# The gate row moved ahead of the scatter for the last two experts of a mixture-of-experts tail

## The chip, the cores and the metric

The kernel runs on one core of a Trainium2 chip. A core has TensorE (PE in the profile, with its weight loads as PEld), VectorE (DVE), ScalarE (ACT), GpSimd (POOL) and SyncE (SP, which issues DMAs), each with a queue of its own that it works off in order. Matmuls write into eight PSUM banks of 128 partitions by 512 floats; everything else lies in SBUF. The metric is the device time of one execution in microseconds.

## The reference, cut to what matters

The model is a two-layer hybrid block on 256 tokens of width 1024, and behind it a second block that ends in a mixture of experts with 16 experts, of which each token uses two. Only the end of it is touched here:

```
x = x + g_f[:, None] * _hier_moe(hf, ...)      # the last operation of the program

out = jnp.zeros_like(t)
for e in range(N_EXPERTS):
    hid = jax.nn.silu(t @ w1[e]) * (t @ w3[e])
    out = out + gate[:, e:e + 1] * (hid @ w2[e])
```

`gate[:, e]` is one number per token and expert. `g_f` is one row of 1024 numbers, the same for every token; the kernel holds it, laid over all partitions, in `gab[:, 1, :]`, and it is called the gate row here. (In the trace `gab` has the name `lnb`, since it shares that buffer.) Since the row doesn't depend on the token, it may be multiplied in before or after rows are handed back to their tokens.

## The kernel before, in words

Every matrix product is made in three matmuls of 32-bit halves: an operand is split into a rounded part (suffix h) and the rest (suffix l), and high by high, low by high and high by low are added in a bank (lines 842, 843 and 844). ScalarE makes the high part of each weight half (line 1602), VectorE the rest (line 2273). The weights stream in through SyncE in a fixed order.

The experts run in chunks, two to an expert (c = 0 to 31, expert x = c // 2). `Walk.experts` sets the order of the work for all engines alike: for a chunk the up products, then the transposed hidden rows of the chunk before (`turn_hidden`, written as `Pall` in the trace), then the down product of the chunk before (`down_part`).

- The first 14 experts (`NFAR`) take their own packed 128 tokens. Their rows go from the bank by ScalarE to `Y[x % 2]`, and GpSimd sends them with an indirect DMA to `ydram`. After chunk 28 GpSimd fetches every token's two possible rows from there (`far`, which is `arena` and `memT` in the trace).
- The last two experts (14 and 15) don't go through DRAM. ScalarE copies the bank to `Yp[0]` (Yph in the trace), VectorE subtracts that from the bank into `Yp[1]` (Ypl), and `scatter(x)` hands both to the tokens by matmuls with a one-hot matrix `back` (line 1566), eight for each expert, into banks 0 to 3: bank 2·hf + t holds columns hf·512 on, of token tile t. Both experts add up in the same banks.
- `combine(t)`, called once behind `down(29)` and once behind `down(30)`, weights and adds the fetched rows of token tile t: ScalarE scales `far[t]` (line 1586), VectorE multiplies and adds (line 2252, the form with two tensors of 128x1024 in SBUF), and GpSimd multiplies by the gate row (line 3327) and adds to `h` (line 3329).

At the end, VectorE multiplies each of the four banks by the gate row into `arena` ("fin"). For the two right halves it adds the product to `h` itself, for the two left halves GpSimd does (line 3333). SyncE stores the four quarters of `h` (line 3413) as they come.

Each engine runs its own queue in the order in which the code is written for it. On VectorE the stretch that matters is: rest of expert 14's rows, `combine(0)`, `Pall` of chunk 30, first half of the last weight tile (`P0l`), hidden rows of chunk 31, second half of `P0l`, `combine(1)`, `Pall` of chunk 31, rest of expert 15's rows, the end.

## Time and profile before

| | us |
|---|---|
| median of 3 runs | 1546.87 (1546.45 to 1547.77) |
| the profiled execution's own time | 1544.67 |
| span of its profile | 1542.9 |
| PE busy in the span | 1515.6 (98%) |
| DVE busy | 1170.5 (76%) |
| ACT busy | 937.8 (61%) |
| POOL busy | 81.0 (5%) |

The span runs from the first to the last thing that the profiler recorded; 1.8 us of the execution lie around it. The stretch that the change touches is the last 26 us, 1517 to 1543. In a timeline a row gives the start and the time of one or several like instructions, and in brackets how long the engine had been idle before it and who ended that. A duration holds the time from issue to end, so an instruction that is held up after it was issued shows as a long one.

### The profile page before, as it was taken

The page shows a single profiled execution, that of the slowest core. Times are in us where ns is not written, and L with a number is a line of the kernel's source. Part 1 is how long each engine was busy: PE and PEld are TensorE (multiplying, and loading weights), DVE is VectorE, ACT ScalarE, POOL GpSimd, SP SyncE. Part 2 cuts the span into 40 slices and gives each one's busy share as a digit, 9 for nine tenths or more (in the row PEclk, how much of TensorE's full clock was granted, in tenths as well). Part 3 has the DMA queues.
Part 4 walks back from the last instruction along what each step waited for, and adds up shares of the span by engine and source line. Part 5 has one row for each costly group of instructions (what it writes and reads, how often), then busy time and mean ns, then how long its engine had stood idle before and what let it go on. Part 6 is the DMA issues. An engine that isn't in the chain of part 4 may idle for free.

```text
span 1542.9 us, 20001 instructions
## 1 busy us (share of the span) xinstructions
PE 1515.6 (98%) x7856; PEld 1257.2 (81%) x7856; DVE 1170.5 (76%) x1623; ACT 937.8 (61%) x1487; POOL 81.0 (5%) x78
## 2 busy tenths in 40 slices
PE   9999999999999999999999999999999889999997
PEld 9988888888888799888888888887777678888785
DVE  7448866667878683688576689886677789999998
ACT  6468854655444354778547554544355468888884
POOL 0010000001000000100000000000200000000005
PEclk9999999999999999999999999999999999999999
DMA  7535345436776444553454468984521349999994
GB/s 294 209 116 215 141 157 195 160 137 260 260 271 246 164 161 168 191 192 137 157 198 178 150 229 316 335 322 161 191 103 55 143 185 367 370 381 384 360 370 169
DMA packets 52200, 339.33 MB, mean 220 GB/s; under 512 B 7835, under 2 KB 8477, under 8 KB 13316
## 3 DMA queue, kind: packets, MB, share of 16 engines
q1 hardware_dynamic: 48932, 331.79, 57.9%
q0 software_dynamic: 3168, 6.20, 1.1%
q8 instruction: 64, 1.05, 0.3%
q14 instruction: 36, 0.29, 0.1%
HBM read 332.82 MB, written 10.49 MB: 223 GB/s over the span
## 4 chain that ended last, share of the span: by engine, by line
PE 88%; DVE 8%; ACT 2%; issue 1%; DMA 1%; POOL 0%; SPq 0%; DVEq 0%; ACTq 0%; POOLq 0%
PE bank L842 25%; PE bank L844 25%; PE bank L843 25%; PE bank L848 5%; DVE wls L2273 2%; PE bank L990 2%; PE bank L1181 1%; PE bank L1379 1%; PE bank L1159 1%; DVE h L2243 1%; PE bank L1098 1%; DMA raw<-in_ws_dram 1%; PE bank L1121 1%; DVE arena L2252 1%; ACT whs L1602 1%
## 5 line engine op out<-in xcount | busy, mean ns | idle before, releaser
L2273 DVE TENSOR_TENSOR wls<-raw,whs 128x1024 fp32r<-128x1024 f32 x424 | 504.2, 1225 | 165.4 <-ACT whs L1602 164.4
L1602 ACT ACTIVATE whs<-raw 128x1024 fp32r<-128x1024 f32 x424 | 427.6, 1051 | 198.6 <-PE bank L844 161.8
L842 PE MATMUL bank<-whs,P1h 128*128 128x512 f32 (+1 forms) x732 | 290.4, 397 | 2.0 <-issue 2.0
L844 PE MATMUL bank<-whs,P1l 128*128 128x512 f32 (+1 forms) x732 | 284.4, 389 | 0.0
L843 PE MATMUL bank<-wls,P1h 128*128 128x512 f32 (+1 forms) x732 | 283.6, 387 | 0.0
L842 PE MATMUL bank<-whs,P0h 128*128 128x512 f32 (+1 forms) x632 | 251.7, 398 | 1.4 <-DVE P0l L2243 1.4
L844 PE MATMUL bank<-whs,P0l 128*128 128x512 f32 (+1 forms) x632 | 245.1, 388 | 0.0
L843 PE MATMUL bank<-wls,P0h 128*128 128x512 f32 (+1 forms) x632 | 244.5, 387 | 0.0
L842 PEld LDWEIGHTS bank<-whs,P1h 128*128 128x128 f32 x732 | 137.6, 188 | 29.7 <-issue 3.3
L844 PEld LDWEIGHTS bank<-whs,P1l 128*128 128x128 f32 x732 | 137.4, 188 | 29.2
L843 PEld LDWEIGHTS bank<-wls,P1h 128*128 128x128 f32 x732 | 137.8, 188 | 26.6
L842 PEld LDWEIGHTS bank<-whs,P0h 128*128 128x128 f32 x632 | 118.8, 188 | 28.2 <-issue 3.1
L844 PEld LDWEIGHTS bank<-whs,P0l 128*128 128x128 f32 x632 | 118.7, 188 | 25.0
L843 PEld LDWEIGHTS bank<-wls,P0h 128*128 128x128 f32 x632 | 118.9, 188 | 23.3 <-issue 0.7
L1586 ACT ACTIVATE arena<-bank 128x256 f32<-128x256 f32 (+2 forms) x132 | 60.8, 467 | 80.7 <-PE bank L844 57.1
L3239 POOL TENSOR_TENSOR sm<-sm,mhalf 128x1 f32<-128x1 f32 (+1 forms) x30 | 26.0, 868 | 977.3 <-DVE sm L2247 854.3
L848 PE MATMUL bank<-ident,arena 128*128 128x128 f32 x410 | 63.9, 274 | 5.1 <-DVE arena L2247 3.8
L2273 DVE TENSOR_TENSOR wls<-landing,whs 128x1024 fp32r<-128x1024 f32 x56 | 66.3, 1219 | 2.3 <-ACT whs L1602 1.8
L848 PEld LDWEIGHTS bank<-ident,arena 128*128 128x128 f32 x410 | 49.5, 141 | 20.4 <-DVE arena L2247 4.8
L1602 ACT ACTIVATE whs<-landing 128x1024 fp32r<-128x1024 f32 x56 | 56.6, 1054 | 4.4 <-PE bank L844 4.4
L842 PE MATMUL bank<-P0h,whs 128*128 128x256 f32 x192 | 55.3, 288 | 0.5 <-DVE wls L2273 0.5
L842 PE MATMUL bank<-P1h,whs 128*128 128x256 f32 x192 | 55.2, 288 | 0.0
(300 smaller groups left out, 2495.8 us busy)
## 6 DMA issues: line engine op xcount, KB each, us to landing
raw<-in_ws_dram SPq DMA_DIRECT2D x264, 1024.0 KB, 4.8
landing<-in_ws_dram SPq DMA_DIRECT2D x38, 1024.0 KB, 6.6
lnb<-in_ln_g_dram SPq DMA_DIRECT2D x6, 512.0 KB, 5.8
lnb<-in_ln_b_dram SPq DMA_DIRECT2D x6, 512.0 KB, 7.0
ydram<-arena POOLq DMA_DIRECT2D x4, 512.0 KB, 8.6
mid<-in_bias_dram SPq DMA_DIRECT2D x1, 2048.0 KB, 9.0
h<-in_x_dram SPq DMA_DIRECT2D x2, 512.0 KB, 3.9
lnb<-in_mem_dram SPq DMA_DIRECT2D x1, 1024.0 KB, 12.2
```

The lines of the kernel that those rows point to most:

```text
L842: e.matmul(out, x[0], w[0], start=start, stop=False, skip_group_check=skip)
L843: e.matmul(out, x[0], w[1], start=False, stop=False, skip_group_check=skip)
L844: return e.matmul(out, x[1], w[0], start=False, stop=stop, skip_group_check=skip)
L848: return e.transpose(out, in_, ident[0:n, 0:n])
L990: m = e.matmul(banks[b][:, ct * 256:ct * 256 + 256], w[:, 2 * b4 + k, ct * 128:(ct + 1) * 128], xc[:, 2 * b4 + k, :], start=k == 0, stop=k ...
L1098: m = e.matmul(banks[4 + o][:, j * w:(j + 1) * w], qT[p:p + 64, hd // 2, t * 128:(t + 1) * 128], kT[p:p + 64, hd // 8, 0:w], start=True, s ...
L1121: m = e.matmul(halves(banks[6][64 * o:64 * o + 64, at:at + 256]), qkv[:, k if t else 0, 1152 + 64 * g:1216 + 64 * g], PT[:, k::2, :] if t ...
L1159: m = e.matmul(banks[b][:, j * 256:(j + 1) * 256], cqT[:, f, t * 128:(t + 1) * 128], ckT[:, f, :], start=k == 0, stop=k == 1)
L1586: e.activation(out, in_, func, bias=bias, scale=scale).then_inc(*act.done(*key))
L1602: e.activation(hi, src, ACT.Copy, bias=0.0, scale=1.0).then_inc(*high.done(n, f))
L2273: e.tensor_tensor(lo, src, f32(hi), ALU.subtract).then_inc(*low.done(n, f))
L3239: e.tensor_tensor(out, in_, mhalf[:, 0:in_.shape[1]], ALU.pow).then_inc(*pool.done(*key))
```

## The change

For experts 14 and 15 VectorE first multiplies the bank by the gate row into `Y[x % 2]` ("yg"), both halves, 512 columns each. ScalarE then takes the high part from `Y`, not from the bank, and VectorE the rest from `Y` and the high part. ScalarE waits for yg where it waited for the bank. The bank is free for TensorE once yg is done.

At the end the four products by the gate row, the two additions of VectorE that followed them and the two additions of GpSimd go. In their place VectorE adds each bank straight to its quarter of `h`, in the order bank 0, 1, 2, 3, and SyncE stores in that order. TensorE's instructions are the same, and so are their number and order.

```
 # vector, down_part, experts 14 and 15
     for hf in range(2):
         b = ((6, 4) if x == NEXP - 1 else (3, 6) if x % 2 else (2, 1))[hf]
         o = slice(hf * 512, (hf + 1) * 512)
+        ve.wait_ge(mm, "edn", c, hf)
+        ve.wait_ge(sent[x % 2], x - 2)
+        ve.wait_ge(vec, "rows", 3)
+        tt(Y[x % 2][:, o], banks[b][:, :], gab[:, 1, o], ALU.mult, "yg", x, hf)
+    for hf in range(2):
+        o = slice(hf * 512, (hf + 1) * 512)
         ve.wait_ge(act, "ey", x, hf)
-        tt(Yp[1][:, o], banks[b][:, :], f32(Yp[0][:, o]), ALU.subtract, "ey", x, hf)
+        tt(Yp[1][:, o], Y[x % 2][:, o], f32(Yp[0][:, o]), ALU.subtract, "ey", x, hf)
 # scalar, down_part, experts 14 and 15
+            ac.wait_ge(vec, "yg", x, hf)
             if x > NFAR:
                 ac.wait_ge(mm, "eacc", x - 1, 1, 1)
-            put(Yp[0][:, o], banks[b][:, :], ACT.Copy, "ey", x, hf)
+            put(Yp[0][:, o], Y[x % 2][:, o], ACT.Copy, "ey", x, hf)
 # vector, behind the last scatter
-    for t in range(2):
-        for n in range(2):
-            s_, o = slice(n * 512, (n + 1) * 512), arr(512 * (2 * n + t), 512)
+    for n in range(2):
+        for t in range(2):
+            s_ = slice(n * 512, (n + 1) * 512)
             ve.wait_ge(mm, "eacc", NEXP - 1, t, n)
-            tt(o, banks[2 * n + t][:, :], gab[:, 1, s_], ALU.mult, "fin", t, n)
-            if n:
-                ve.wait_ge(vec, "fin", t, n)
-                ve.wait_ge(pool, "h", t)
-                tt(h[:, t, s_], h[:, t, s_], o, ALU.add, "out", t, n)
+            ve.wait_ge(pool, "h", t)
+            tt(h[:, t, s_], h[:, t, s_], banks[2 * n + t][:, :], ALU.add, "out", t, n)
 # gpsimd, behind the two additions of combine
-    for t in range(2):
-        po.wait_ge(vec, "fin", t, 0)
-        po.wait_ge(pool, "h", t)
-        e.tensor_tensor(h[:, t, 0:512], h[:, t, 0:512], arr(512 * t, 512), ALU.add).then_inc(*pool.done("out", t, 0))
 # sync
-    for t in range(2):
-        for n in range(2):
-            sp.wait_ge((pool, vec)[n], key, t, n)
+    for n in range(2):
+        for t in range(2):
+            sp.wait_ge(by[n], key, t, n)
```

VectorE's queue around expert 14's rows, before. `Ypl` is the rest of the rows, the 128x1024 operation on `arena` is `combine(0)`, `Pall` the hidden rows of chunk 30, `P0l` the last weight tile:

```order
L2273 TENSOR_TENSOR wls<-raw,whs 128x1024 x2
L2243 TENSOR_TENSOR Ypl<-bank,Yph 128x512 x2
L2252 SCALAR_TENSOR_TENSOR arena<-arena,sm 128x1024
L2243 TENSOR_TENSOR Pall<-bank,Pall 128x256
L2273 TENSOR_TENSOR P0l<-raw,P0h 128x1024
L2252 SCALAR_TENSOR_TENSOR arena<-arena,sm,bank 128x256
L2273 TENSOR_TENSOR P0l<-raw,P0h 128x1024
```

The same place in the changed kernel, whose lines stand one further down:

```order
L2274 TENSOR_TENSOR wls<-raw,whs 128x1024 x2
L2244 TENSOR_TENSOR Y<-bank,lnb 128x512 x2
L2244 TENSOR_TENSOR Ypl<-Y,Yph 128x512 x2
L2253 SCALAR_TENSOR_TENSOR arena<-arena,sm 128x1024
L2244 TENSOR_TENSOR Pall<-bank,Pall 128x256
L2274 TENSOR_TENSOR P0l<-raw,P0h 128x1024
L2253 SCALAR_TENSOR_TENSOR arena<-arena,sm,bank 128x256
L2274 TENSOR_TENSOR P0l<-raw,P0h 128x1024
```

Two instructions have come in ahead of `Ypl`, and `Ypl` has two inputs in SBUF where one was a bank. In ScalarE's queue the two copies stand where they stood, ahead of its part of `combine(0)`, and only their input and their wait are others.

VectorE's queue at the end of the program, before, from `combine(1)` (on `memT`) on:

```order
L2252 SCALAR_TENSOR_TENSOR memT<-memT,sm,arena 128x1024
L2243 TENSOR_TENSOR Pall<-bank,Pall 128x256
L2243 TENSOR_TENSOR Ypl<-bank,Yph 128x512 x2
L2243 TENSOR_TENSOR arena<-bank,lnb 128x512 x2
L2243 TENSOR_TENSOR h<-h,arena 128x512
L2243 TENSOR_TENSOR arena<-bank,lnb 128x512 x2
L2243 TENSOR_TENSOR h<-h,arena 128x512
```

And in the changed kernel:

```order
L2253 SCALAR_TENSOR_TENSOR memT<-memT,sm,arena 128x1024
L2244 TENSOR_TENSOR Pall<-bank,Pall 128x256
L2244 TENSOR_TENSOR Y<-bank,lnb 128x512 x2
L2244 TENSOR_TENSOR Ypl<-Y,Yph 128x512 x2
L2244 TENSOR_TENSOR h<-h,bank 128x512 x4
```

Behind the last scatter four instructions stand where there were six, all of them with one input in a bank; ahead of it there are four where there were two, and both products by the gate row stand ahead of both rests.

## Rows read from the trace of the kernel before

**Rows 1.** The page: each engine's busy time, share and instructions.
```profile
PE 1515.6 (98%) x7856; PEld 1257.2 (81%) x7856; DVE 1170.5 (76%) x1623; ACT 937.8 (61%) x1487; POOL 81.0 (5%) x78
```

**Rows 2.** Chain that ended last, 1519 to 1543: start us, us, what.
```profile
1522.73 2.44 issue
...
1526.51 2.02 issue
```

**Rows 3.** Timeline of VectorE, 1517 to 1543: start us, us, instruction, idle before.
```profile
1519.20 1.28 DVE L2243 TENSOR_TENSOR Ypl<-bank,Yph 128x512 fp32r<-128x512 f32 x2
1520.40 1.28 DVE L2252 SCALAR_TENSOR_TENSOR arena<-arena,sm 128x1024 f32<-128x1024 f32 x1
...
1522.70 2.56 DVE L2273 TENSOR_TENSOR P0l<-raw,P0h 128x1024 fp32r<-128x1024 f32 x1 [0.53 <-ACT P0h L1602]
1525.18 0.47 DVE L2252 SCALAR_TENSOR_TENSOR arena<-arena,sm,bank 128x256 f32<-128x256 f32 x1
1525.57 3.04 DVE L2273 TENSOR_TENSOR P0l<-raw,P0h 128x1024 fp32r<-128x1024 f32 x1
...
1529.73 0.41 DVE L2243 TENSOR_TENSOR Pall<-bank,Pall 128x256 fp32r<-128x256 f32 x1
...
1533.98 0.69 DVE L2243 TENSOR_TENSOR Ypl<-bank,Yph 128x512 fp32r<-128x512 f32 x1 [0.70 <-ACT Yph L1586]
...
1535.50 0.69 DVE L2243 TENSOR_TENSOR arena<-bank,lnb 128x512 f32<-128x512 f32 x1 [0.23 <-PE bank L1566]
...
1538.40 1.26 DVE L2243 TENSOR_TENSOR h<-h,arena 128x512 f32<-128x512 f32 x1
```

**Rows 4.** Timeline of GpSimd in the same stretch.
```profile
1521.76 2.41 POOL L3327 TENSOR_TENSOR arena<-arena,lnb 128x1024 f32<-128x1024 f32 x1 [4.31 <-DVE arena L2252]
1524.25 3.27 POOL L3329 TENSOR_TENSOR h<-h,arena 128x1024 f32<-128x1024 f32 x1
...
1532.34 2.39 POOL L3329 TENSOR_TENSOR h<-h,memT 128x1024 f32<-128x1024 f32 x1
...
1537.85 1.26 POOL L3333 TENSOR_TENSOR h<-h,arena 128x512 f32<-128x512 f32 x1 [1.23 <-DVE arena L2243]
```

**Rows 5.** Timeline of ScalarE in the same stretch.
```profile
1517.73 1.22 ACT L1586 ACTIVATE Yph<-bank 128x512 fp32r<-128x512 f32 x2
1518.85 1.15 ACT L1586 ACTIVATE arena<-arena,sm 128x1024 f32<-128x1024 f32 x1
...
1531.96 0.60 ACT L1586 ACTIVATE Yph<-bank 128x512 fp32r<-128x512 f32 x1 [4.48 <-PE bank L844]
1533.35 0.60 ACT L1586 ACTIVATE Yph<-bank 128x512 fp32r<-128x512 f32 x1 [0.80 <-PE bank L844]
```

**Rows 6.** Timeline of TensorE in the same stretch.
```profile
1523.88 0.40 PE L842 MATMUL bank<-whs,Pall 128*128 128x512 f32 x1
...
1526.81 0.48 PE L1566 MATMUL bank<-Yph,Back 128*128 128x512 f32 x1
...
1530.28 0.47 PE L842 MATMUL bank<-P0h,Pall 128*128 128x512 f32 x1 [1.38 <-DVE Pall L2243]
...
1533.33 0.50 PE L1566 MATMUL bank<-Yph,Back 128*128 128x512 f32 x1
...
1534.72 0.50 PE L1566 MATMUL bank<-Yph,Back 128*128 128x512 f32 x1 [0.19 <-DVE Ypl L2243]
```

**Rows 7.** Groups of VectorE by line and shape, whole span: count, busy us, mean ns, idle before.
```profile
L2243 DVE TENSOR_TENSOR P0l<-end,P0h 128x512 fp32r<-128x512 f32 x8 | 5.5, 685 | 4.7 <-ACT P0h L1586 4.7
```

**Rows 8.** Groups of ScalarE by line and shape, 1240 to 1543, same columns.
```profile
L1586 ACT ACTIVATE P1h<-arena 128x640 fp32r x16 | 11.7, 731 | 0.9 <-DVE arena L2258 0.9
L1586 ACT ACTIVATE P1h<-memT 128x384 fp32r x16 | 8.3, 516 | 1.3 <-DVE memT L2258 1.3
```

**Rows 9.** Windows: us, busy (count) of PE, PEld, DVE, ACT, POOL, granted clock, DMA, GB/s.
```profile
1216.00:1219.00 3.00, 0.77 (x6) 0.39 (x5) 2.23 (x6) 0.00 (x0) 0.55 (x1) 1.00 0.82 328
...
1538.00:1540.00 2.00, 0.00 (x0) 0.00 (x0) 1.63 (x2) 0.00 (x0) 1.11 (x1) 0.60 0.52 188
```

More of the change, by code:

```diff
@@ L1549, in down_part @@
                             if i == 0 and k == 0:
-                                bank(b, (act if x < NFAR else vec, "ey", x, hf))
+                                bank(b, (act, "ey", x, hf) if x < NFAR else (vec, "yg", x, hf))
                             m = mm3(banks[b][:, :], part_of(hid, slice(None), 2 * i + k),
@@ L1563, in scatter @@
                             if x == NFAR:
-                                bank(b, (vec, "fin", t, hf))
+                                bank(b, (vec, "out", t, hf))
                             for p in range(2):
@@ L2208, in down_part @@
                         o = slice(hf * 512, (hf + 1) * 512)
-                        ac.wait_ge(mm, "edn", c, hf)
-                        wait_for(start)
                         if x < NFAR:
+                            ac.wait_ge(mm, "edn", c, hf)
+                            wait_for(start)
                             if x >= 2:
@@ L3407, in sync, with stores @@
             weights(main)
-            def stores(key):
-                for t in range(2):
-                    for n in range(2):
-                        sp.wait_ge((pool, vec)[n], key, t, n)
+            def stores(key, by):
+                for n in range(2):
+                    for t in range(2):
+                        sp.wait_ge(by[n], key, t, n)
                         e.dma_start(outs[0][0, t * 128:(t + 1) * 128, n * 512:(n + 1) * 512],
@@ L3419, in sparse @@
                 weights(list(paths[1]))
-                stores("out")
+                stores("out", (vec, vec))
             def dense():
                 weights(list(paths[0]))
-                stores("dout")
+                stores("dout", (pool, vec))
             two_ways(sp, None, sparse, dense)
```

## The prediction

> **What bounds the kernel now.** I read the page first. TensorE is busy 98% of the span [rows 1], which ends at 1542.9 us, and the change leaves its instructions alone. So it can move the time only where TensorE waits, or behind its last matmul. For that I read the chain of waits over the last 24 us, then each engine's timeline there. The reader is to see two things.
>
> First, the chain leaves TensorE at the start of the last weight tile and runs through VectorE, with two stretches in which VectorE is said to wait for nothing, 2.44 and 2.02 us [rows 2]. They lie inside the two `P0l` instructions, which take 2.56 and 3.04 us [rows 3]. What they wait for is seen beside GpSimd's rows: its product runs to 1521.76 + 2.41 = 1524.17, and the first `P0l` ends 1.09 later, at 1525.26. GpSimd's addition, issued at 1524.25, takes 3.27 in place of the 2.39 of its twin, so it too was held, until that `P0l` was through; it ends at 1527.52, and the second `P0l` ends 1.09 later, at 1528.61 [rows 3, 4]. The last `h<-h,arena` does the same: GpSimd's last addition ends at 1539.11, VectorE's ends 0.55 later, at 1539.66. Instructions with one input in a bank aren't held: the hidden rows (0.47) and `Ypl` (0.69) run inside GpSimd's instructions [rows 3, 4]. So in this trace a VectorE instruction with two tensors in SBUF and a GpSimd tensor instruction exclude each other, whoever is in first, for its whole length.
>
> Second, this locked sequence has a fixed length. From the end of `combine(0)` on VectorE (1520.40 + 1.28 = 1521.68), which releases GpSimd's product, to the first matmul of the last down product (1530.28) it is 8.60 us, and TensorE stands idle 1.38 us for it [rows 3, 6]. Then come down product, rows to `Yp`, scatter, and VectorE's end work until 1539.66; the last store and its landing take the 3.2 us from there to 1542.9.
>
> **The change, part by part, in the profile's own time.**
>
> Expert 15 and the end, first with everything ahead unmoved. The down product's first half is ready at 1531.96, its second at 1533.35 [rows 5].
> - yg: a bank and an SBUF tensor in, as in `arena<-bank,lnb` (0.69) and the old `Ypl` (0.69, 1.28 for two) [rows 3], so 0.69 each and 0.6 apart. The first at 1531.96 to 1532.65. The second needs the second half: 1533.35 to 1534.04. They aren't held.
> - Yph from `Y`: ScalarE's rows from SBUF are 516 ns at 384 columns and 731 at 640 [rows 8]; between them lies 0.62 at 512, against 0.60 from the bank. It overlaps.
> - Ypl from `Y` and Yph: 0.69 alone (685 ns for two SBUF inputs [rows 7]). The first now stands behind the second yg, at 1534.0, and is of the held form: GpSimd's last big addition runs until 1534.73 [rows 4]. So it ends 0.55 later, at 1535.28. The second ends at 1535.9.
> - The scatter's first half starts at 1535.3, where it was 1533.33 [rows 6]: the term that the change pays here. From the start of a half to VectorE's use of its first bank it is 0.78 (1534.72 to 1535.50 [rows 3, 6]).
> - The end: four additions bank + `h`, one input in a bank, so again 0.69 and 0.6 apart: 1536.1 + 0.69 + 3 x 0.6 = 1538.6. TensorE's second half, starting at about 1536.3, delivers in time (the twelve matmuls from 1530.28 to 1533.33 took 0.25 each at most [rows 6]). Against 1539.66 that is 1.05 us gained: work behind the scatter shrinks by some 3.0, and 1.95 of it go to the later scatter.
>
> Expert 14, behind `down(29)`. Its bank rows are long ready; VectorE gets there at 1519.20 and ScalarE was there already at 1517.73 [rows 3, 5]. Before, ScalarE ran ahead: two copies and its part of `combine(0)` by 1518.85 + 1.15 = 1520.00, so VectorE never waited. Now it has to follow VectorE:
> - yg 1519.20 to 1519.88 and 1520.48 (two in 1.28).
> - Yph 1519.92 to 1520.54 and 1521.15.
> - ScalarE's part of `combine(0)`, 1.15, in order behind it: 1521.06 to 1522.2.
> - VectorE: Ypl to 1521.27 and 1521.85 beside that (no GpSimd tensor instruction runs yet); then `combine(0)` waits for ScalarE: 1522.24 to 1523.52.
>
> So `combine(0)` ends at 1523.52 instead of 1521.68: 1.84 us late. Ends for it: with 0.52 or 0.73 for a Yph it is 1.6 to 2.1. Everything behind moves along, since the locked sequence of 8.60 us starts there. GpSimd's product starts at 1523.6, `Pall` of chunk 30 (0.41) runs 1523.44 to 1523.85, and the first `P0l` comes at 1523.77, after GpSimd has the lock, so it is held again until 1526.0. Before, it came 0.94 after GpSimd (1521.76, 1522.70 [rows 3, 4]), now 0.17. What TensorE needs meanwhile: `Pall` of chunk 30 was used at 1523.88 [rows 6], so it is just in time, with 0 to 0.1 lost. The hidden rows of chunk 31 come at 1525.65 + 1.84 = 1527.5; TensorE turned them and began expert 14's scatter by 1526.81 [rows 6], so it now idles some 0.8 there. That scatter's eight matmuls then end near 1529.8, ahead of 1532.1, so both waits are inside the one that follows. The last down product starts at 1523.52 + 8.60 = 1532.12 in place of 1530.28. From there all of the paragraph on expert 15 moves as a whole, GpSimd's additions too, since they hang on `combine(1)` in the same sequence.
>
> Sum: +1.84 - 1.05 = +0.8 us. The profiled execution took 1544.67, so 1545.5; it lay 2.2 below the median of the three runs, and the same difference on the median 1546.87 gives 1547.7. SyncE's store order changes nothing: each store waits for an addition that is 0.6 after the one before, and the last one ends the span as before.
>
> The form Ypl<-Y,Yph beside GpSimd stands in no row; I price it by `P0l` and `h<-h,arena`. If it were not held, the first would end at 1534.7, 0.6 sooner, and the sum would be +0.2. The Trainium skill (SBUF — State Buffer, section "SBUF: two separate sides") says that VectorE with two SBUF inputs against a GpSimd instruction that reads SBUF is an exclusive lock for the whole instruction, whatever the tensors; by it the sum stays at +0.8, and the four rows above agree to 0.01 us with each other (1.09 twice, 0.55 twice at half the columns).
>
> Of the input moved from bank to SBUF, the rows say nothing changes on VectorE: 685 ns from SBUF [rows 7] against 0.69 from the bank [rows 3]. The Trainium skill (VectorE: DVE Perf Modes, section "The TRN2 errata") tables a fixed 58 cycles from SBUF and 120 from PSUM on VectorE, 224 and 172 on ScalarE. By that, as an estimate, each Ypl would be 0.06 shorter and each Yph 0.04 longer, and the sum still 0.8; for VectorE the trace doesn't agree, and I take the trace.
>
> **The rivals.**
> 1. The delay of `combine(0)` doesn't reach TensorE (ends the other way: faster). The gain at the end, 1.05, stands alone: 1545.8. It decides where the delay is under 1.05 us. For it: VectorE is the later of the two now (ScalarE's part ends 0.4 before `combine(0)` starts), so ScalarE has slack, and only what is beyond it counts. Against it: my sum has used that slack up, and TensorE's 1.38 us of idle time already hang on this very sequence.
> 2. VectorE wins the lock. `P0l` comes only 0.17 us after GpSimd's product in my sum. If the ends of the range put it first, it runs at once, GpSimd's product follows 1.1 later, and the second `P0l` is held once, not twice in a row: the down product could start up to 1.9 sooner (1545.9), or, if GpSimd's addition then gets in ahead of `combine(1)`, 0.6 later than in the sum (1548.3). Against it: GpSimd is released by the end of `combine(0)`, and `Pall` (0.41) stands before `P0l`.
> 3. TensorE's clock falls in the longer waits. In my sum TensorE stands still from 1529.8 to 1532.1 and again from 1535.3 to 1537.2. The granted clock was 1.00 through 1216 to 1219, where TensorE was busy 0.77 of 3 us; it fell to half only behind the program's last matmul (0.60 as the mean of 1538 to 1540) [rows 9]. The price has no row here: twelve down and eight scatter matmuls, 0.25 us apart, are at most doubled, 20 x 0.25 = 5.0 on top of the forecast, and at least nothing: 1547.7 to 1552.7, taken at the middle, 1550.2. The Trainium skill (TensorE: Matmul & The Clock Gate, "Part 1: The HAM clock gate") says that the clock is granted by how busy TensorE has been recently; the trace agrees in that it fell after the work had ended, and by that rule alone I can't exclude a fall here.
>
> **How the numbers follow.** The forecast, +0.8, has 0.62; its own range from the bounds (0.6 or not for Ypl, 1.6 to 2.1 for the delay, +-0.7 for the scatter of medians, seen as 1546.45 to 1547.77) is 1546.6 to 1548.8. Rival 1 has 0.17, rival 2 0.11, rival 3 0.06; 0.04 is for what I don't see. Eight in ten: from 1545.6, in rival 1's reach, to 1549.6. A measurement of this kernel tells about 0.2%, 3.1 us, from no change. Forecast, rivals 1 and 2 are all within it. Slower by more takes rival 3 at its upper part or a miss of mine: 0.05. Faster by more takes something that isn't here: 0.02. Within: 0.93.
>
> **What would show it.** Right: in the changed profile `combine(0)` on VectorE ends about 1.8 us later and waits for ScalarE; the first `P0l` is about 3.3 us long, held to the end of GpSimd's product; TensorE idles about 2.4 us ahead of the last down product; the first Ypl of expert 15 is longer than 0.69; four additions of 0.69 end the program, some 0.8 later than 1539.66. Wrong: `combine(0)` late by under 1 us, a last down product that starts near 1530.3, a Ypl of 0.69 beside a running GpSimd addition, or a granted clock under 1.00 before the last matmul.

## The result, and the profile after

Median of 22 executions of each kernel, on one chip:

| | before | changed |
|---|---|---|
| median, us | 1546.91 | 1549.39 |
| lowest and highest | 1544.83, 1548.20 | 1547.73, 1551.57 |
| span of the profiled execution | 1542.9 | 1546.9 |
| end of VectorE's last addition | 1539.66 | 1542.74 |

Changed over before is 1.0016, 95% interval [1.0009, 1.0022]: slower by 2.5 us, where +0.8 had been forecast. 1549.39 lies just inside the eight-in-ten range (to 1549.6) and inside the 0.2%, but above the sum's own range (1546.6 to 1548.8), and the interval leaves out the forecast's 1.0005. So 1.7 us have to be found.

The work itself is what it was. The page, as in [rows 1]:

```profile
PE 1517.8 (98%) x7856; PEld 1258.2 (81%) x7856; DVE 1172.7 (76%) x1625; ACT 937.6 (61%) x1487; POOL 79.3 (5%) x76
```

The timeline of VectorE from expert 14's rows on, which answers to [rows 3] (start us, us, instruction, idle before it and its releaser):

```profile
1520.48 1.28 DVE L2244 TENSOR_TENSOR Y<-bank,lnb 128x512 f32<-128x512 f32 x2
1521.86 1.29 DVE L2244 TENSOR_TENSOR Ypl<-Y,Yph 128x512 fp32r<-128x512 f32 x2
1523.57 1.28 DVE L2253 SCALAR_TENSOR_TENSOR arena<-arena,sm 128x1024 f32<-128x1024 f32 x1 [0.41 <-ACT arena L1586]
1524.77 0.42 DVE L2244 TENSOR_TENSOR Pall<-bank,Pall 128x256 fp32r<-128x256 f32 x1
1525.11 3.32 DVE L2274 TENSOR_TENSOR P0l<-raw,P0h 128x1024 fp32r<-128x1024 f32 x1
1528.35 0.47 DVE L2253 SCALAR_TENSOR_TENSOR arena<-arena,sm,bank 128x256 f32<-128x256 f32 x1
1528.74 3.00 DVE L2274 TENSOR_TENSOR P0l<-raw,P0h 128x1024 fp32r<-128x1024 f32 x1
...
1535.09 0.69 DVE L2244 TENSOR_TENSOR Y<-bank,lnb 128x512 f32<-128x512 f32 x1 [1.82 <-PE bank L844]
...
1537.10 1.91 DVE L2244 TENSOR_TENSOR Ypl<-Y,Yph 128x512 fp32r<-128x512 f32 x2
1539.48 0.69 DVE L2244 TENSOR_TENSOR h<-h,bank 128x512 f32<-128x512 f32 x1 [0.48 <-PE bank L1566]
...
1542.05 0.69 DVE L2244 TENSOR_TENSOR h<-h,bank 128x512 f32<-128x512 f32 x1 [0.17 <-PE bank L1566]
```

VectorE comes to expert 14's rows at 1520.48, where it was 1519.20. That 1.28 us lies ahead of every changed instruction and differs from execution to execution (over the kernels below the point lies between 1519.2 and 1521.7). Part of that is the clock: in seven of the thirteen traces the granted clock is at 0.50 for a stretch near 1219 or 1253 too (e3, e4, e5, e6, e8, e10 and e11), and VectorE is here at 1520.3 to 1521.7 in them, at 1519.2 to 1520.5 in the six others. So from here on each trace is counted from that point, called **T0**. Against T0 the rows answer the forecast one by one. `combine(0)` waits 0.41 for ScalarE and ends at T0 + 4.37, before at T0 + 2.48: 1.89 later (1.84 had been forecast). The first `P0l` comes 0.17 us after GpSimd's product (1525.11 and 1524.94 below) and is 3.32 long, held until 1.09 after that product's end at 1527.34. GpSimd in the same stretch, as in [rows 4]:

```profile
1524.94 2.40 POOL L3331 TENSOR_TENSOR arena<-arena,lnb 128x1024 f32<-128x1024 f32 x1 [4.70 <-DVE arena L2253]
```

And ScalarE:

```profile
1521.20 1.23 ACT L1586 ACTIVATE Yph<-Y 128x512 fp32r<-128x512 f32 x2 [2.08 <-DVE Y L2244]
1522.33 1.14 ACT L1586 ACTIVATE arena<-arena,sm 128x1024 f32<-128x1024 f32 x1
```

TensorE at the places of [rows 6]:

```profile
1528.87 0.44 PE L848 MATMUL bank<-ident,arena 128*128 128x128 f32 x2 [0.54 <-DVE arena L2253]
...
1533.42 0.47 PE L842 MATMUL bank<-P0h,Pall 128*128 128x512 f32 x1 [2.27 <-DVE Pall L2244]
...
1538.46 0.56 PE L1566 MATMUL bank<-Yph,Back 128*128 128x512 f32 x1 [2.01 <-DVE Ypl L2244]
1538.82 0.63 PE L1566 MATMUL bank<-Ypl,Back 128*128 128x512 f32 x1
1539.24 0.63 PE L1566 MATMUL bank<-Yph,Back 128*128 128x512 f32 x1
...
1541.38 0.63 PE L1566 MATMUL bank<-Ypl,Back 128*128 128x512 f32 x1
```

The last down product starts at T0 + 12.94, before at T0 + 11.08: 1.86 later. Then comes what had been left to a rival: the last scatter's eight matmuls stand 0.43 apart where 0.23 is this kernel's spacing, and the granted clock falls with them. Windows of 1 us (us, busy and count of PE, PEld, DVE, ACT, POOL, granted clock, DMA, GB/s):

```profile
1537.00:1538.00 1.00, 0.00 (x0) 0.00 (x0) 1.00 (x2) 0.63 (x1) 0.85 (x1) 1.00 0.00 0
1538.00:1539.00 1.00, 0.54 (x2) 0.47 (x3) 1.00 (x2) 0.00 (x0) 0.00 (x0) 0.88 0.02 8
1539.00:1540.00 1.00, 1.00 (x4) 0.81 (x3) 0.52 (x2) 0.00 (x0) 0.00 (x0) 0.50 0.00 0
```

The last addition ends at T0 + 22.26, before at T0 + 20.46. And the tail from there to the end of the span, which had been carried over as 3.2 us, is 1546.9 - 1542.7 = 4.2. What SyncE waited for at the end (total, times, longest) in the changed kernel:

```profile
SPq L148 <- DMA out_dram<-h: 3.1, 1, 3.1
```

And in the kernel before:

```profile
SPq L148 <- DMA out_dram<-h: 1.7, 1, 1.7
```

So the changed span is 4.0 us longer: 1.3 ahead of the change, 1.8 between T0 and the last addition, 1.0 behind it. The median shows 2.5, near the last two together.

### The profile page after: what moved, and what is told of

It reads as the page before. It is cut to its first block, busy times and chain, and to the rows that moved or that the text cites. A ratio compares the mean times of both kernels' runs of the same rounds, so it can differ in the third digit from the quotient of the medians.

```text
span 1546.9 us, 20001 instructions
## 1 busy us (share of the span) xinstructions
PE 1517.8 (98%) x7856; PEld 1258.2 (81%) x7856; DVE 1172.7 (76%) x1625; ACT 937.6 (61%) x1487; POOL 79.3 (5%) x76
## 3 DMA queue, kind: packets, MB, share of 16 engines
q8 instruction: 64, 1.05, 0.3%
## 4 chain that ended last, share of the span: by engine, by line
PE 87%; DVE 8%; ACT 2%; DMA 1%; issue 1%; POOL 0%; SPq 0%; DVEq 0%; ACTq 0%; POOLq 0%
PE bank L842 25%; PE bank L844 25%; PE bank L843 24%; PE bank L848 5%; DVE wls L2274 3%; PE bank L990 2%; DMA raw<-in_ws_dram 1%; PE bank L1181 1%; PE bank L1379 1%; PE bank L1159 1%; PE bank L1098 1%; DVE h L2244 1%; PE bank L1121 1%; DVE arena L2253 1%; ACT whs L1602 1%
```

## The experiments

Every kernel is counted from T0 in its own profile. D is T0 to the end of VectorE's last addition, the tail is what follows, and the two spans at the right are T0 to the end of the span against before's 23.7, and the measured ratio times 1547 less 1547. Each profile is one execution, each ratio comes from interleaved runs.

| kernel | last down product | D | tail | T0 to end, against before | ratio [95%] | as us |
|---|---|---|---|---|---|---|
| before | 11.08 | 20.46 | 3.2 | 0 | | |
| changed | 12.94 | 22.26 | 4.2 | +2.7 | 1.0016 [1.0009, 1.0022] | +2.5 |
| e1 expert 14 plain | 11.08 | 19.37 | 5.8 | +1.5 | 1.0004 [0.9995, 1.0013] | +0.6 |
| e2 expert 14 only | 12.95 | 22.33 | 3.5 | +2.1 | 1.0010 [1.0001, 1.0019] | +1.5 |
| e3 ScalarE's part first | 12.45 | 21.23 | 5.4 | +2.9 | 1.0012 [1.0003, 1.0021] | +1.9 |
| e4 fillers, 16 and 14 | 14.01 | 23.15 | 5.1 | +4.5 | 1.0020 [1.0011, 1.0030] | +3.1 |
| e5 e1, small stores | 11.1 | 19.37 | 5.8 | +1.5 | 1.0005 [0.9996, 1.0014] | +0.8 |
| e6 before, late stores | 11.51 | 20.90 | 5.4 | +2.6 | 1.0016 [1.0007, 1.0025] | +2.5 |
| e7 fillers, 8 and 7 | 12.95 | 21.24 | 5.4 | +2.9 | 1.0018 [1.0008, 1.0027] | +2.8 |
| e8 no GpSimd sums | | 17.33 | 5.8 | -0.6 | 1.0002 [0.9992, 1.0011] | +0.3 |
| e9 e7, TensorE ends late | 12.95 | 21.25 | 5.1 | +2.6 | 1.0019 [1.0010, 1.0028] | +2.9 |
| e10 before, sums on VectorE | | 19.18 | 3.5 | -1.0 | 0.9988 [0.9979, 0.9997] | -1.9 |

The two views of the whole, from one profile and from the ratios, agree within 1.5 us on every row. Read D beside the tail: what a kernel wins in D mostly goes again in the tail. e1 wins 1.1 and loses 2.6.

**e1: expert 14 as before, expert 15 and the end as changed.**

```diff
-    for hf in range(2):
+    for hf in range(2 if x > NFAR else 0):
...
-        tt(Yp[1][:, o], Y[x % 2][:, o], f32(Yp[0][:, o]), ALU.subtract, "ey", x, hf)
+        tt(Yp[1][:, o], banks[b][:, :] if x == NFAR else Y[x % 2][:, o], f32(Yp[0][:, o]), ALU.subtract, "ey", x, hf)
```

The first loop is VectorE's product by the gate row; ScalarE's copies and waits go back in the same way. The gate row is missing from expert 14's part of the result.

> The changed kernel with expert 14's rows handled as before (copied from the bank, not multiplied by the gate row; that factor is left out for expert 14). Theory: the 1.84 us by which combine(0) came late, and with it 1.9 us of the start of the last down product, go; TensorE's wait ahead of it is 1.4 us again, the wait ahead of the last scatter stays 2.0, the clock stays at 1.00 until that scatter is through. Last VectorE addition about 1.0 sooner than in the kernel before; the four stores now lie closer together, so the span gains less: 0.0 to 0.7 us faster than before (1546.9), 2.5 to 3 faster than the change. Rival (the end costs it: later scatter, half clock, crowded stores): it stays 1 us or more slower than before.

The delay is gone: last down product at T0 + 11.08 as before, to the hundredth, behind TensorE's old wait (timeline of TensorE).

```profile
1530.87 0.47 PE L842 MATMUL bank<-P0h,Pall 128*128 128x512 f32 x1 [1.38 <-DVE Pall L2247]
...
1535.91 0.50 PE L1566 MATMUL bank<-Yph,Back 128*128 128x512 f32 x1 [2.01 <-DVE Ypl L2247]
```

Its VectorE at the end:

```profile
1536.68 2.48 DVE L2247 TENSOR_TENSOR h<-h,bank 128x512 f32<-128x512 f32 x4 [0.22 <-PE bank L1566]
```

D is 1.09 shorter than before's, where 1.05 had been worked out for the end work. Here TensorE kept its clock in the last scatter (0.23 apart) behind the same wait of 2.01. But the time isn't 1 us better than before: the ratio's interval, 0.8 us faster to 2.0 slower, leaves a gain of 1.1 out, and the tail is 5.8. That was the first sign of the step that failed.

**e2: expert 14 as changed, expert 15 and the end as before.**

```diff
+    for hf in range(2 if x == NFAR else 0):
+        ...
+        tt(Y[x % 2][:, o], banks[(2, 1)[hf]][:, :], gab[:, 1, o], ALU.mult, "yg", x, hf)
```

> The kernel before with one part of the change alone: expert 14's rows multiplied by the gate row ahead of their split (its rows then carry that factor twice), the end as before. Theory: combine(0) 1.84 us late, TensorE's wait ahead of the last down product 2.3 in place of 1.4, everything behind 1.8 us later: 1548.7, with up to 2 us more in executions in which the granted clock falls in that wait. Rival: no change against before, 1546.9.

The timeline of its VectorE, at `combine(0)`:

```profile
1522.60 1.28 DVE L2255 SCALAR_TENSOR_TENSOR arena<-arena,sm 128x1024 f32<-128x1024 f32 x1 [0.41 <-ACT arena L1586]
```

TensorE:

```profile
1532.45 0.47 PE L842 MATMUL bank<-P0h,Pall 128*128 128x512 f32 x1 [2.26 <-DVE Pall L2246]
```

The same 0.41, the same 2.26 ahead of the down product, D longer by 1.87 and a tail of 3.5: slower by 1.5 us, interval above 1. The forecast's +1.84 stands alone here, and it agrees: it lies in that interval, 0.2 to 2.9 us. Two of the eleven executions, not profiled, took 1550.6 and 1551.0 at a mean granted clock of 0.996 and 0.995, the nine others 1547.2 to 1549.1 at 0.998 and 0.999; so here too the clock may fall in some.

**e3: ScalarE's part of `combine(0)` moved ahead of its two copies.**

```diff
+    if c == last - 1 and early:
+        combine(0)
```

> The changed kernel with one ScalarE instruction moved: its part of combine(0) stands ahead of the two copies of expert 14's rows. Same result. Theory: ScalarE does it in the 2 us in which it waits for VectorE, combine(0) on VectorE no longer waits for it (0.41 us idle gone) and ends some 0.45 us sooner; TensorE's wait ahead of the last down product 1.8 in place of 2.27; 0.5 us faster than the change, 1548.9. Rival (the handover is not on the path): same as the change.

The timeline of its ScalarE:

```profile
1520.51 1.15 ACT L1588 ACTIVATE arena<-arena,sm 128x1024 f32<-128x1024 f32 x1 [0.18 <-DMA arena<-ydram,idx]
```

And of its VectorE:

```profile
1523.08 1.29 DVE L2247 TENSOR_TENSOR Ypl<-Y,Yph 128x512 fp32r<-128x512 f32 x2
1524.29 1.28 DVE L2256 SCALAR_TENSOR_TENSOR arena<-arena,sm 128x1024 f32<-128x1024 f32 x1
```

`combine(0)` no longer waits, it starts at T0 + 2.60 instead of 3.09, and the down product comes 0.49 sooner (12.45). So of the 1.9 us of delay 0.5 is the handover and 1.4 is what VectorE itself has taken on: the two products by the gate row in front. TensorE's wait ahead of the last down product stayed 2.27, where 1.8 had been expected: what was gained came off the wait ahead of the turn of the hidden rows (0.25 in place of 0.54). The ratio, 1.0012, can't be told from the changed kernel's.

**e4 and e7: matmuls by a constant tile in TensorE's two waits, so that it isn't still.** The change with 16 and 14 of them, then with 8 and 7:

```diff
+    if c == 2 * NEXP - 1:
+        keep_up(5, 8)      # e4: 16
...
+    if x > NFAR:
+        keep_up(5, 7)      # e4: 14
```

> The changed kernel with 16 filler matmuls (ones by ones, 128 columns, 0.12 us apart, into a free bank) in TensorE's wait ahead of the last down product and 14 in the wait ahead of the last scatter. Same result. Theory: the granted clock stays 1.00 until the last scatter is through; its matmuls are 0.23 apart in place of 0.43, VectorE's last addition comes 1.0 us sooner; the stores then lie 0.6 apart and queue behind each other, so the span gains 0.4 to 1.0: 1548.4 to 1549.0, and the spread between executions shrinks. Rival (the stores alone set the end from the first addition on, the clock costs nothing): same as the change, 1549.4.

> The changed kernel with 8 and 7 filler products (each is two passes of 0.11 us, 0.23 together, where e4's 16 and 14 ran past the end of the waits they were to fill). Theory: no matmul of the program starts later for them, the granted clock is 1.00 until the last scatter is through, its matmuls are 0.23 apart, VectorE's last addition comes 1.0 us sooner than in the profile of the change (21.3 us behind its start on expert 14's rows in place of 22.3); but the stores now crowd as in e1 and give most of it back: 1548.6 to 1549.4 against 1549.4. Rival (clock and stores add up): 1548.4.

TensorE's timeline in e4:

```profile
1530.92 3.73 PE L828 MATMUL bank<-allone 128*128 128x128 f32 x32
```

And in e7:

```profile
1529.99 1.95 PE L828 MATMUL bank<-allone 128*128 128x128 f32 x16
1532.42 0.47 PE L842 MATMUL bank<-P0h,Pall 128*128 128x512 f32 x1 [0.49 <-DVE Pall L2248]
...
1537.47 0.50 PE L1570 MATMUL bank<-Yph,Back 128*128 128x512 f32 x1 [0.45 <-DVE Ypl L2248]
1537.80 0.39 PE L1570 MATMUL bank<-Ypl,Back 128*128 128x512 f32 x1
```

e4 was a mistake of size: each filler is two instructions of 0.11 us, so twice as much went in as had been reckoned. The down product starts 1.07 us later than in the changed kernel, the last scatter 1.9 later than in e7 (T0 + 19.92 and 18.00). Its 1.0020 says nothing of the clock. e7 fits: waits of 0.49 and 0.45 are left, the scatter keeps 0.23, and D is 21.24, the forecast's 20.46 + 0.8 = 21.26. So the clock cost the profiled changed kernel 22.26 - 21.24 = 1.0 us in D. The time didn't follow, 1.0018: the tail was 5.4. The profiled execution of e7, 1547.93 at a mean granted clock of 1.000, is one of the three shortest of eleven; nine had 0.997 or 0.998, so its profile doesn't show how most of them went.

**e5: e1 with three of the four stores cut to 64 columns** (the output's other columns of these three quarters are not written). By now the tail was the question, and my theory was that four stores released 0.6 us apart crowd one another, 1.8 us from the first to the last, where before it was 3.0.

```diff
-    e.dma_start(outs[0][0, t * 128:(t + 1) * 128, n * 512:(n + 1) * 512],
-                h[:, t, n * 512:(n + 1) * 512])
+    w = 512 if t and n else 64
+    e.dma_start(outs[0][0, t * 128:(t + 1) * 128, n * 512:n * 512 + w],
+                h[:, t, n * 512:n * 512 + w])
```

> The kernel of e1_expert14_plain with the first three of the four stores cut to 64 of their 512 columns (so the rest of those quarters isn't stored); the last store is whole. In e1 VectorE's last addition came 1.1 us sooner (counted from its start on expert 14's rows) but the span ended 5.9 us behind it, against 3.2 in the kernel before. Theory: the four stores, asked for within 2 us, share the DMA engines, and the last one lands 4.4 us after its issue instead of 2.3; with the others small it lands in 2.3, the span ends 3.2 behind the last addition, and e1's gain shows: 1545.7 to 1546.4, about 1.2 to 2.5 faster than e1. Rival (something else at the program's end is longer): as e1, 1547.4.

SyncE's wait at the end:

```profile
SPq L148 <- DMA out_dram<-h: 4.1, 1, 4.1
```

The theory fell. With 0.36 MB to carry instead of 1.05, the tail stayed at 5.8 and the ratio at e1's; 1.2 to 2.5 us had been expected.

**e6: the kernel before, its four stores all held back until the last additions.**

```diff
+    sp.wait_ge(vec, key, 1, 1)
+    sp.wait_ge(pool, key, 1, 0)
```

> The kernel before with one wait more: SyncE waits for the last two additions ahead of its first store, so that all four are asked for within 1.2 us. Nothing else is changed and the output is the same. Theory: VectorE's last addition stays, the span ends 5 to 6.5 us behind it in place of 3.2: 1548.9 to 1550.2. A share of it is the plain transfer of 1 MB at 370 GB/s (2.8 us), and what is beyond that is the slow end of crowded stores. Rival (stores are short against the end): 1 us at most, 1547.9.

Its SyncE:

```profile
1541.90 2.00 SPq L3415 DMA_DIRECT2D out_dram<-h  x4
```

Here 1 MB leaves behind the last addition: tail 5.4, slower by 2.5 us. Most of that is the row of issues: the last store is issued at 1543.5, 1.6 us behind the last addition (before: at once), and its last packet ends 2.8 us after that (before: 2.1). So stores do cost when all of them are late, but e5 shows that their bytes aren't what makes e1's tail. Its D contains 0.34 us of a wait of `combine(0)` for the fetched rows, which is not the edit's; the tail doesn't.

**What the tail is.** The DMA row of the last 6 us, 1539 to 1545 (GB/s in 40 slices of 0.15 us), of e1:

```profile
GB/s 41 41 82 0 27 55 341 396 382 423 314 396 396 423 328 369 396 355 328 369 14 55 0 0 0 0 14 14 14 0 27 27 14 0 0 0 0 0 0 0
```

And of before, 1537 to 1543:

```profile
GB/s 0 0 0 246 355 382 396 396 342 410 396 382 191 109 0 0 55 0 0 82 341 314 410 382 151 41 150 396 410 382 355 82 55 0 0 0 0 0 0 0
```

In e1 the bulk is through at slice 22 (1542.3), then nothing, then from 1542.9 a trickle at 14 to 27, one packet at a time; the span ends 1.1 us behind it. Before has no trickle. The packets' own records, which no view prints, name it. They hold 64 packets of 16 KB of the kind `instruction` in a queue of their own (q8), in every trace. I take them for TensorE's instruction stream, loaded by DMA: in e9 below, where TensorE alone is made to end later, they come later with it. Two such loads start late in every trace, in all but e9 the first 0.2 to 1.9 us ahead of the end of TensorE's last matmul and the second 3.3 to 4.9 us after the first. Put on the span's clock (zero is the first instruction's start in each trace):

| | second code load | end | next packet of the last store | last store's last data packet |
|---|---|---|---|---|
| before | 1539.06 + 1.06 | 1540.11 | none held | 1541.80 |
| changed | 1543.80 + 0.98 | 1544.78 | 1544.78, eight in a row | 1545.74 |
| e1 | 1541.93 + 0.98 | 1542.92 | 1542.90, eight in a row | 1543.93 |
| e5 | 1543.25 + 0.93 | 1544.18 | 1544.16, eight in a row | 1545.19 |
| e7 | 1542.98 + 1.01 | 1543.99 | 1543.97, eight in a row | 1545.00 |
| e8 | 1540.00 + 1.32 | 1541.32 | 1541.30, eight in a row | 1542.33 |
| e3 | 1545.66 + 0.93 | 1546.59 | 1546.58, its closing packet alone | 1545.94 |

A store is 128 packets, eight for each of 16 DMA engines. In all these but before, and in e4 and e11 too, the packets of one sixteenth of the last store, or its closing one of 4 bytes, start within 0.02 us of the end of TensorE's code load. That they stand behind it in one DMA engine is read from these times; the record doesn't name the engine. In e1 all others had landed by 1542.2, so it costs 1.8 us there; in e5 2.3; in the changed kernel, whose last store came later, 0.6. In before, e2, e6 and e10 the load is over while the last store is only beginning.

The loads are felt in SyncE's issues of the stores as well. From the views of their line (ns least, median and most, then first and last start), in e1:

```profile
L3417 SPq DMA_DIRECT2D out_dram<-h x4: 348/469/1402, 1537.4 to 1540.0; - x4
```

And in e9, whose loads come later:

```profile
L3418 SPq DMA_DIRECT2D out_dram<-h x4: 332/338/347, 1539.3 to 1541.1; - x4
```

An issue takes 0.33 to 0.35 us in e9 and 1.40 in e1, where the load ran from 1537.54 to 1539.05 and the second issue, begun at 1537.99, ended at 1539.39. So it is in eleven of the thirteen traces: the store issue that meets such a load takes 0.6 to 1.4 us and ends 0.32 to 0.38 behind the load's end (in before, e2, e6 and e10 it is the second load, in the seven others the first). In e1, e5, e7 and e8 the issue so held is the second, and the last store is asked for 0.6 to 1.0 us behind the last addition instead of at once. e1's tail is then made up of 0.8 to that issue, 2.2 until all but the held packets have landed, 1.8 for these, and 1.1 to the end of the span; before's of 0.0, 2.1, none and 1.1. By these figures the two loads account for all that the one has over the other. In the changed kernel it is 0.0, 2.4, 0.6 and 1.1.

**e8: the change, with GpSimd's products and additions of the fetched rows left out** (the fetched rows of all experts are missing from the result; waits and signals are left out of the lines here).

```diff
-    e.tensor_tensor(b, b, gab[:, 1, :], ALU.mult)
-    e.tensor_tensor(h[:, t, :], h[:, t, :], b, ALU.add)
+    e.tensor_copy(b[:, 0:2], b[:, 0:2])
```

> The changed kernel with GpSimd's two products by the gate row and its two additions to h left out (two copies of two columns stand for them, so the fetched rows are missing from the result). Theory (VectorE's two-SBUF-input instructions and GpSimd's exclude each other): both P0l take 1.22 us in place of 3.32 and 3.00, the two Ypl of expert 15 take 1.29 together in place of 1.91, TensorE's wait ahead of the last down product is under 0.5 us in place of 2.27, VectorE's last addition comes 4 to 5 us sooner and the clock stays at 1.00: 1544 to 1545.5. Rival (P0l is slow for its input or the wait for ScalarE): P0l stays near 3 us and the time near 1549.

VectorE's timeline:

```profile
1524.91 1.22 DVE L2274 TENSOR_TENSOR P0l<-raw,P0h 128x1024 fp32r<-128x1024 f32 x1
1526.04 0.48 DVE L2253 SCALAR_TENSOR_TENSOR arena<-arena,sm,bank 128x256 f32<-128x256 f32 x1
1526.52 1.23 DVE L2274 TENSOR_TENSOR P0l<-raw,P0h 128x1024 fp32r<-128x1024 f32 x1
...
1533.64 1.47 DVE L2244 TENSOR_TENSOR Ypl<-Y,Yph 128x512 fp32r<-128x512 f32 x2
```

The two `P0l` take 1.22 and 1.23 instead of 3.32 and 3.00, and the pair of `Ypl` 1.47 instead of 1.91. D falls by 4.9 us against the changed kernel's profile. 1.0 of that is the clock, which stayed at 1.00 through the last scatter here; against e7, with the same work at the full clock, it is 21.24 - 17.33 = 3.9. That is the hold (the two `P0l` alone are 2.10 and 1.77 shorter), and nothing else was changed around it. The Trainium skill (SBUF — State Buffer, section "SBUF: two separate sides") calls it an exclusive lock for a VectorE instruction with two SBUF inputs against a GpSimd one that reads SBUF, and the trace agrees: 1.09 us behind GpSimd's end with the lock, 1.22 in all without a rival for it. Of D's 4.9 us the time shows 2.2 (1.0002 against 1.0016): the tail is 5.8.

**e9: e7, with TensorE made to wait at its end for VectorE's last addition,** so that its last code loads come later than the last store.

```diff
+    pe.wait_ge(vec, "out", 1, 1)
```

> The kernel of e7_fillers_8_7 with one wait more: behind its last scatter TensorE waits for VectorE's last addition before it leaves the sparse part. The reason: in the five traces in which the span ends 4.2 to 5.8 us behind the last addition in spite of small or whole stores, eight packets of the last store start within 0.02 us of the end of TensorE's second 16 KB code load (queue q8), one behind the other, 0.9 to 1.7 us after the other 120; in the kernel before that load (3.3 us behind the first, which comes with the last matmul) is over before the last store's packets start. Theory: the wait moves both loads by 1.5 us or more, behind the last store's packets; none of them straggles; the last store lands in about 2.5 us in place of 4.0, and the span ends about 4.2 behind the last addition in place of 5.4, unless TensorE's own late end sets it: 1548.6 to 1549.2 against 1549.8. Rival (stragglers come from something else in the stores): tail and time as in e7.

SyncE's waits at the end:

```profile
SPq L148 <- DMA out_dram<-h: 2.8, 1, 2.8
SPq L486 <- PEq L486: 1.5, 1, 1.5
```

The held packets are gone, and so is the long issue: the first load now starts at 1543.45 (in e7 at 1539.38), behind all four issues, the last data packet ends at 1543.90, the second load starts at 1546.55, behind the span's end, and the last store lands in 3.1 us, in e7 4.0. But now SyncE waits 1.5 us for TensorE's end, where it was 0.2 in every other kernel, and the time is e7's, 1.0019. So moving the loads took the held packets away, which supports that the loads held them, but ending TensorE late doesn't pay: TensorE's own end is the next thing behind.

**e10: the kernel before, GpSimd's products and additions of the fetched rows given to VectorE.** This follows from e8: 4.9 us of VectorE work (four instructions of 1.22) in place of the hold, put where VectorE waited. Waits are left out of the lines here.

```diff
+    def scaled(t):
+        tt(far[2 + t], far[2 + t], gab[:, 1, :], ALU.mult, "far", t)
+    def added(t):
+        tt(h[:, t, :], h[:, t, :], far[2 + t], ALU.add, "h", t)
...
+    if c == 2 * NEXP - 1:
+        scaled(0)          # behind the first P0l; added(0), scaled(1) behind the last Pall,
+                           # added(1) between the two Ypl of expert 15
```

> The kernel before (not the change) with the fetched rows' product by the gate row and their addition to h moved from GpSimd to VectorE, into places where it was idle or held: the first product between the two P0l, one addition and one product behind the last Pall, the last addition between the two Ypl of expert 15. Same result. Theory (GpSimd's hold on VectorE is what TensorE waits for): both P0l take 1.22, TensorE's wait of 1.38 ahead of the last down product is under 0.1, that product starts 1.3 sooner and the last addition comes 0.5 to 1.2 us sooner (19.3 to 20.0 behind VectorE's start on expert 14's rows in place of 20.5); stores as far apart as before, so the span keeps it: 1545.7 to 1546.4 against 1546.9. Rival (VectorE's own 4.9 us of new work outweigh the hold): later last addition, 1548 or more.

VectorE's timeline:

```profile
1524.41 1.23 DVE L2273 TENSOR_TENSOR P0l<-raw,P0h 128x1024 fp32r<-128x1024 f32 x1 [0.53 <-ACT P0h L1602]
1525.56 1.22 DVE L2243 TENSOR_TENSOR arena<-arena,lnb 128x1024 f32<-128x1024 f32 x1
1526.69 0.47 DVE L2252 SCALAR_TENSOR_TENSOR arena<-arena,sm,bank 128x256 f32<-128x256 f32 x1
1527.17 1.23 DVE L2273 TENSOR_TENSOR P0l<-raw,P0h 128x1024 fp32r<-128x1024 f32 x1
```

TensorE's 1.38 us ahead of the last down product are gone, D is 1.28 shorter, the tail stays short at 3.5: 0.9988 [0.9979, 0.9997], 1.9 us faster than before, and the only kernel here that beats it. The interval goes from 0.5 to 3.2 us; 0.5 to 1.2 had been expected.

**e11: the changed kernel once more,** one execution, to see whether its clock falls again.

> The changed kernel itself, once more for its trace alone. Theory: the handover (0.41 us of VectorE's wait for ScalarE ahead of combine(0)), the two held P0l (3.3 and 3.0), the wait of 2.27 ahead of the last down product and the one of 2.0 ahead of the last scatter are the same to 0.05 us; where the granted clock falls in or ahead of the last scatter may be elsewhere, and with it 0 to 2 us of the span.

TensorE's timeline in the last scatter:

```profile
1538.88 0.40 PE L1566 MATMUL bank<-Yph,Back 128*128 128x512 f32 x1
1539.12 0.56 PE L1566 MATMUL bank<-Ypl,Back 128*128 128x512 f32 x1
1539.48 0.63 PE L1566 MATMUL bank<-Yph,Back 128*128 128x512 f32 x1
```

It fell again, from the fourth matmul of the last scatter on: D is 21.78, half a microsecond over e7's. Its tail is 5.3: the closing packet of its last store starts at the code load's end, 0.6 us behind the last data packet. T0 isn't the only thing in which two executions of one kernel differ. T0 to the end is 27.1, +3.4.

## Why the prediction was right in kind and short by 1.7 us

- **ScalarE now follows VectorE, and `combine(0)` is 1.84 late.** Right: 1.89 in the changed kernel, with 0.41 of wait (forecast 1522.24 - 1521.85 = 0.39). e2 shows it alone, e1 removes it, e3 splits it.
- **It reaches TensorE through the locked sequence.** Right: 12.94 against 11.08, TensorE idle 2.27 (forecast 2.4) and 0.54 ahead of the turn of the hidden rows (forecast 0.8). The hold is shown by e8. Rival 1, that the delay stays off TensorE, is out. Rival 2, VectorE first, didn't happen: GpSimd was first by the forecast 0.17 us.
- **The end work shrinks by more than the scatter is later, -1.05.** Right: -1.09 in e1, D of 21.24 in e7 against 21.26.
- **The clock stays at 1.00.** Wrong in both profiled executions of the changed kernel and in e3's: the granted clock went to 0.50 in the last scatter, behind waits of 2.27 and 2.01. It was rival 3, with 0.06. Its price was mis-sized too, 2.5 us at the middle: the down product kept the full clock, only the last scatter paid, 1.0 and 0.5 us. e1 had the one wait of 2.01 behind one of 1.38 and kept its clock. The Trainium skill (TensorE: Matmul & The Clock Gate, "Part 1: The HAM clock gate") had the direction: the clock is granted by recent activity. That the earlier wait decides isn't shown: e5, with 1.38 and 2.02, kept its clock as e1 did, but no kernel was profiled more than twice, and the fall began at the first matmul of the scatter in one trace and at the fourth in two. How long a pause this kernel can bear isn't settled by these rows.
- **"SyncE's store order changes nothing ... the last one ends the span as before", the 3.2 us.** This step failed. The tail is a race between the stores and what I take for TensorE's last two code loads, and the change brings them together: the last addition now ends 0.7 us behind the last matmul (1541.38 + 0.63 = 1542.01 to 1542.74) instead of 3.7. The tail was 4.2 and 5.3 in the changed kernel's two profiles, 3.2 before, 3.5 in the two kernels with the old end (e2, e10), and 5.1 to 5.8 in those with the new end and a full clock. In other words, the 1.05 us that the end work gives back is lost again, and more, as e1 shows: +0.6 on the clock of the time, not -1.1.

The 1.7 us that were missing are thus clock (0.5 to 1.0) and tail (1.0 to 2.1). They don't add up exactly, and can't from single profiles: with the clock fallen the last store is later and is held less, so the two overlap. Nor is any one profile the median: the mean granted clock of the 22 executions is 0.995 in three, which took 1550.5 to 1551.6, and 0.998 in five, which took 1548.4 to 1549.4, the profiled one among them. A lower clock goes with more time, but that mean also counts falls near 1219 and 1253 and behind the last matmul, so how often the clock falls in the last scatter stays open. That the result lies in the eight-in-ten range is in part luck: the range was wide enough for a step that had been put at nothing. (Rival 2's 1545.9 is 1545.8 by its own terms; nothing rests on it.)

## What to carry to other kernels

Before you shorten the work behind the last matmul, look at what else ends the program there: the span ended 1.1 us behind the last store's last data packet in ten of the thirteen traces (in e3 and e11 the closing packet was late and the span ended 1.7 behind it; in e9 TensorE's end was later), and a code load can hold that packet and the issue of a store. A product put ahead in VectorE's order, with ScalarE made to follow it, delays everything behind it in both queues, so read whom the next instruction releases. Where VectorE's instructions with two SBUF inputs last longer than their twins, count what GpSimd holds; giving VectorE the same sums (4 times 1.22 us) was worth 1.9 us here, though it added work to the busier engine.

## What the runs showed that I had not expected

- Code is loaded during the run by DMA (TensorE's, as I read it), 16 KB in 0.93 to 1.5 us near the end. Packets of the last store start within 0.02 us of such a load's end and are through 0.6 to 2.3 us behind the rest of it, and an issue of SyncE that meets a load ends 0.32 to 0.38 us behind it.
- A wait of 2.0 us ahead of eight matmuls halved the granted clock in all three profiles in which a wait of 2.27 had gone before it (changed, e3, e11), and not in e1 and e5, where 1.38 had. That is a count over five profiles, not a rule that was tested. Nor did it fall in e2, with 2.26 and then 0.20. In the changed kernel the fall took the spacing from 0.23 to 0.43 us.
- The input's place made no difference to ScalarE or VectorE at 512 columns: two `Yph` from SBUF 1.23, from the bank 1.22 [rows 5]; two `Ypl` from SBUF 1.29, from the bank 1.28 [rows 3]. The Trainium skill (VectorE: DVE Perf Modes, "The TRN2 errata") tables different fixed costs for the two; these rows don't show them.
